# DeltaNet with unnormed keys: the keys' norm carried by beta and the values, the products of keys and queries three steps sooner

## The reference

```python
qkv = jax.nn.silu(centred_depthwise_conv(qkv, conv_w))      # 5 taps
q = l2norm(q.reshape(b_, s_, h_, HEAD_DIM)) * (HEAD_DIM ** -0.5)
k = l2norm(k.reshape(b_, s_, h_, HEAD_DIM))
beta = jax.nn.sigmoid(bt)
# chunk_gated_delta, forward and backward, chunks of tokens:
kb = k * beta[..., None]
a_low = jnp.where(strict, jnp.einsum("bhnid,bhnjd->bhnij", kb, k) * decay, 0.0)
rhs = jnp.concatenate([v * beta[..., None], kb * jnp.exp(gc)[..., None]], axis=-1)
sol = solve_triangular(a_low + eye, rhs)
attn = jnp.einsum("bhnid,bhnjd->bhnij", q, k) * decay
k_dec = k * jnp.exp(g_last - gc)[..., None]
...
o = rmsnorm(o_f + o_b, out_g) * silu(z)
```

## Time and profile before

| what | value |
|---|---|
| median of 3 runs | 2374.19 us (2373.24 to 2380.41) |
| the profiled execution's own time | 2374.28 us |
| its span, first to last instruction | 2372.5 us |
| mean granted TensorE clock | 0.998 |
| VectorE's first taps of k in groups 0, 1 and 2 | 167.30, 335.63, 504.91 us |

### The profile page before, as it was taken

One profiled execution on the slowest core, in us unless ns is written; L12 is line 12 of the kernel. 1 busy time (PEld: TensorE's weight loads), 2 busy tenths in 40 slices (PEclk: granted clock), 3 DMA queues, 4 the chain that ended last, 5 costly groups with the idle time before them and its releaser, 6 DMA issues.

```text
span 2372.5 us, 36123 instructions
## 1 busy us (share of the span) xinstructions
PE 2340.4 (99%) x11982; PEld 1982.2 (84%) x11982; DVE 1537.0 (65%) x2457; ACT 1250.9 (53%) x2326; POOL 159.9 (7%) x120
## 2 busy tenths in 40 slices
PE   8999999999999999999999999999999999999998
PEld 6887888988888888888888888888888888888886
DVE  6668778678676765556665565556676555676554
ACT  6656556565455554445554455555555444455544
POOL 0012002011001000001000000000111000011000
PEclk9999999999999999999999999999999999999999
DMA  9565355353366665666666666556666666666665
GB/s 335 156 169 151 107 143 142 107 177 98 103 177 189 189 191 193 194 188 186 186 189 193 193 208 172 162 184 197 185 185 186 194 193 191 186 186 186 194 192 172
DMA packets 234264, 423.00 MB, mean 178 GB/s; under 512 B 27532, under 2 KB 35613, under 8 KB 233501
## 3 DMA queue, kind: packets, MB, share of 16 engines
q1 hardware_dynamic: 234141, 421.33, 59.4%
HBM read 419.14 MB, written 2.10 MB: 178 GB/s over the span
## 4 chain that ended last, share of the span: by engine, by line
PE 94%; DVE 4%; ACT 1%; DMA 1%; issue 0%; SPq 0%; POOLq 0%; DVEq 0%; POOL 0%; ACTq 0%
PE pair L519 18%; PE pair L521 18%; PE pair L520 18%; PE pair L538 10%; PE aux L538 10%; PE aux L540 5%; PE pair L540 5%; PE aux L710 4%; PE aux L567 2%; DVE r L1768 1%; DVE w_lo L1540 1%; DMA raw<-in_mem_w_kv 1%; PE aux L750 0%; DVE r L1841 0%; PE aux L686 0%; PE aux L669 0%
## 5 line engine op out<-in xcount | busy, mean ns | idle before, releaser
L1540 DVE TENSOR_TENSOR w_lo<-raw,w_hi 128x512 fp32r<-128x512 f32 x1536 | 1090.8, 735 | 615.5 <-ACT w_hi L1026 613.1
L1026 ACT ACTIVATE w_hi<-raw 128x512 fp32r<-128x512 f32 x1536 | 938.6, 633 | 767.4 <-DMA raw<-in_ffn_w 626.6
L519 PE MATMUL pair<-w_hi,xT 128*128 128x512 f32 x960 | 386.9, 403 | 13.7 <-DVE w_lo L1540 10.4
L519 PE MATMUL pair<-w_hi,hid_hi 128*128 128x512 f32 x1012 | 394.4, 390 | 0.0
L521 PE MATMUL pair<-w_hi,hid_lo 128*128 128x512 f32 x1012 | 393.9, 389 | 0.0
L520 PE MATMUL pair<-w_lo,hid_hi 128*128 128x512 f32 x1012 | 393.7, 389 | 0.0
L521 PE MATMUL pair<-w_hi,xT 128*128 128x512 f32 x960 | 375.3, 391 | 0.0
L520 PE MATMUL pair<-w_lo,xT 128*128 128x512 f32 x960 | 374.6, 390 | 0.0
L538 PE MATMUL pair<-xT,w_hi 128*128 128x512 f32 x1024 | 362.6, 398 | 0.4 <-DVE h L2030 0.2
L538 PE MATMUL aux<-xT,w_hi 128*128 128x512 f32 x1024 | 360.8, 397 | 0.0
L540 PE MATMUL aux<-xT,w_lo 128*128 128x256 f32 x1024 | 287.4, 281 | 0.0
(11 more groups left out here) (244 smaller groups left out, 1593.8 us busy)
## 6 DMA issues: line engine op xcount, KB each, us to landing
raw<-in_ffn_w SPq DMA_DIRECT2D x1024, 256.0 KB, 3.0
raw<-in_dn_w_in SPq DMA_DIRECT2D x208, 256.0 KB, 2.9
raw<-in_tok_w_out SPq DMA_DIRECT2D x128, 256.0 KB, 3.0
raw<-in_gm_w_in SPq DMA_DIRECT2D x112, 256.0 KB, 2.9
raw<-in_mem_w_kv SPq DMA_DIRECT2D x64, 256.0 KB, 3.6
r<-in_mem_columns SPq DMA_DIRECT2D x8, 256.0 KB, 6.6
h<-in_x_columns SPq DMA_DIRECT2D x2, 1024.0 KB, 7.4
h<-in_mem_columns SPq DMA_DIRECT2D x8, 256.0 KB, 3.6
```

Of the source, the lines that this page charges most:

```text
L519: pe.matmul(acc, act_hi[:, kt, tokens], w_hi[:, slot], start=start, stop=False)
L1026: act.activation(w_hi[:, slot], raw[:, slot], ACT.Copy).then_inc(hi_ready, 1)
L1540: dve.tensor_tensor(w_lo[:, slot], raw[:, slot], w_hi[:, slot].bitcast(F32), ALU.subtract).then_inc(tiles_split, 1)
```

## The change

Keys stay unnormed. k after `silu` goes straight to `kqT`, and its transpose to tokens is used where normed k was. With r = 1 / (sum of squares of k + eps), `means` takes the reciprocal and multiplies beta by r; the values are multiplied by the root of the sum (`head_root`, GpSimd's power 1/2, used in `scaled_values` by VectorE, where ScalarE copied them). `decayed_keys` multiplies the unnormed keys by their decay out of the bank on VectorE, where VectorE wrote the normed keys and GpSimd scaled them. The transposes DE and their copies are gone. The gate products DF and the products DG come three steps sooner, the masking (L1835, L1841) is spread over two steps, and the taps of k and q over more steps in groups 0 and 1. The transposes of q and its squares move behind level 4 (`Q_LEVEL`, `DQ`), `query_term` to the end. `mix_pairs(2, 3)` stands behind the transposes DH. GpSimd's additions L2230 wait for half of k's squares and stand ahead of its power. A group has three steps fewer, and `ALONE` is `(22,)`.

```diff
 ORDER = (1, 0, 2)
-DA, DD, DE, DF, DG, DH, DI = 0, 6, 10, 12, 16, 20, 24
-V_LEVEL = 2
+DA, DD, DF, DG, DH, DI = 0, 6, 8, 12, 16, 20
+V_LEVEL, Q_LEVEL = 2, 4
 DV = DI + 6 * (V_LEVEL + 1)
-DFT = DI + 6 * len(LEVELS) + 2
+DQ = DI + 6 * (Q_LEVEL + 1) + 2
+DFT = DI + 6 * len(LEVELS) + 4
 DWV = DFT + 4
 DST, DO1, DKS, DQS, DWR, DO2 = DWV + 4, DWV + 6, DWV + 8, DWV + 10, DWV + 12, DWV + 14
...
-DMA0, DMA2 = DD + 2, DF
+DMA0, DMA2 = DF, DI
...
-ALONE = (19, 21, 23, 25)
+ALONE = (22,)
...
-                    src = kqT[:, 0] if X == 0 else conv[X]
+                    src = kqT[:, X] if X < 2 else conv[X]
...
                 mix_pairs(0, 1)
                 yield
-                yield
-                by_tokens(0, DD + 2)
-                yield
-                for _ in range(1 * roomy):
-                    yield
-                for m in range(2):
-                    have(DD + m)
-                for hp in range(2):
-                    pair_transposes(at(DE + hp), tok[:, 1], hp, rnd)
-                yield
-                mix_pairs(2, 3)
                 for f in range(4):
                     fill(DF + f)
                     pe.wait_ge(sem("gates_spread"), g * 4 + (f + 1))
@@ -751,8 +741,6 @@
                                    start=True, stop=True), DF + f)
                 yield
-                for n in range(2):
-                    have(DE + n)
                 pe.wait_ge(sem("silu_done"), g * 3 + 2)
                 for m in range(2):
                     for hp in range(2):
@@ -765,18 +753,16 @@
                         done(mm, n)
                 yield
                 yield
-                for d in range(2):
-                    for m in range(2):
-                        have(DG + 2 * m)
-                        have(DG + 2 * m + 1)
-                        transposes(at(DH + 2 * d + m), [(k * P, NT[:, d, m, k, :]) for k in range(4)], rnd)
-                yield
-                yield
                 for _ in range(1 * roomy):
                     yield
+                for m in range(2):
+                    have(DG + 2 * m)
+                    have(DG + 2 * m + 1)
+                    for d in range(2):
+                        transposes(at(DH + 2 * m + d), [(k * P, NT[:, d, m, k, :]) for k in range(4)], rnd)
+                yield
+                mix_pairs(2, 3)
+                yield
...
+                    if l == Q_LEVEL:
+                        by_tokens(0, DQ)
...
-                    pe.wait_ge(sem("kdec_done"), g * 2 + (d + 1))
+                    have(DD + d)
...
-                    if X == 2:
+                    if X == 2 and not roomy:
                         silu(1)
                     yield
+                if roomy:
+                    silu(1)
                 yield
                 for _ in range(1 * roomy):
                     yield
-                squares(1, (sq[:, 0], sq[:, 1]), DD)
+                squares(1, DD)
                 yield
                 mix_pairs(0, 1)
                 yield
                 silu(0)
-                yield
-                squares(0, v_new, DD + 2)
-                yield
-                for _ in range(1 * roomy):
-                    yield
-                for hp in range(2):
-                    n = DE + hp
-                    fil(n)
-                    free(act.activation(kqT[:, 1, 2 * hp:2 * hp + 2, :], halves(n), ACT.Copy), n)
-                attention_part()
-                yield
-                mix_pairs(2, 3)
                 for f in range(4):
                     drained(act, at(DF + f), rnd)
                     act.activation(NT[:, f // 2, f % 2], NT[:, f // 2, f % 2], ACT.Exp).then_inc(sem("decay_ready"), 1)
                 yield
                 yield
-                yield
+                attention_part()
+                yield
+                for _ in range(1 * roomy):
+                    yield
...
+                mix_pairs(2, 3)
+                yield
...
-                    if l == V_LEVEL:
-                        for m in range(2):
-                            fil(DV + m)
-                            free(act.activation(tok[:, 2, m], bank(DV + m)[:], ACT.Copy), DV + m)
+                    if l == Q_LEVEL:
+                        squares(0, DQ)
...
                     dve.tensor_scalar(ss[:, 1], ss[:, 1], 1.0, EPS, ALU.mult, ALU.add).then_inc(sem("head_means"), 1)
+                    dve.wait_ge(sem("head_means"), g + 1)
+                    dve.reciprocal(rs[:, 0], ss[:, 1]).then_inc(sem("head_inverse"), 1)
+                    dve.wait_ge(sem("head_inverse"), g + 1)
+                    dve.wait_ge(sem("group_gates"), g + 1)
+                    betas = gs[:, 2 * G_BETA:2 * G_BETA + 4, :].rearrange("p (m d) h -> p m d h", d=2)
+                    dve.tensor_tensor(betas, betas, rs[:, 0].unsqueeze(2).broadcast_to([P, 2, 2, 4]), ALU.mult
+                                      ).then_inc(sem("betas_scaled"), 1)
...
-                def normalise():
-                    dve.wait_ge(sem("head_rstd"), g + 1)
+                def decayed_keys():
+                    for d in range(2):
+                        n = DD + d
+                        fil(n)
+                        free(dve.tensor_tensor(kdec[d], heads(n), rows(gs[:, 2 * (G_EKD + d) + d, :], P), ALU.mult), n)
+                def scaled_values():
+                    dve.wait_ge(sem("head_root"), g + 1)
                     for m in range(2):
-                        n = DD + m
-                        free(dve.tensor_tensor(by_head(tok[:, 1, m]), heads(n), rows(rs[:, 1, m], P), ALU.mult), n)
+                        n = DV + m
+                        fil(n)
+                        free(dve.tensor_tensor(v_tok[m], heads(n), rows(rs[:, 1, m], P), ALU.mult), n)
                 dve.wait_ge(sem("padded"), g * 2 + 2)
                 convolve(1, 0, 1)
                 yield
-                convolve(1, 2, 3)
-                yield
-                convolve(0, 0, 1)
-                yield
-                convolve(0, 2)
-                yield
-                for _ in range(1 * roomy):
+                if roomy:
+                    convolve(1, 2)
+                    yield
+                    convolve(1, 3)
+                else:
+                    convolve(1, 2, 3)
+                yield
+                for i in range(3):
+                    convolve(0, i)
                     yield
                 convolve(0, 3)
+                mix_pairs(0, 1)
                 yield
                 means()
-                mix_pairs(0, 1)
-                yield
-                normalise()
-                yield
-                yield
-                for _ in range(1 * roomy):
-                    yield
-                query_term()
-                attention_part()
-                yield
-                mix_pairs(2, 3)
+                decayed_keys()
                 for f in range(4):
...
-                dve.wait_ge(sem("head_squares1"), g * 8 + 8)
+                dve.wait_ge(sem("betas_scaled"), g + 1)
...
+                    if m == 1:
+                        attention_part()
+                    yield
+                for _ in range(1 * roomy):
+                    yield
+                for m in range(2):
+                    n = DH + 2 * m
...
+                    if l == V_LEVEL:
+                        scaled_values()
...
+                query_term()
...
-                pool.wait_ge(sem("head_means"), g + 1)
-                pool.tensor_tensor(flat(rs[:, 1]), flat(ss[:, 1]), neg_half[:], ALU.pow).then_inc(sem("head_rstd"), 1)
+                pool.wait_ge(sem("head_squares1"), g * 8 + 4)
                 for f in range(4):
                     d, m = f // 2, f % 2
                     c = (C_BIGF, C_BIGB)[d]
                     pool.tensor_tensor(g_big[:, f], over(cst[:, c:c + P]), heads(gall[:, 2 * (G_GC + m) + d, g * 4:g * 4 + 4]), ALU.add
                                        ).then_inc(sem("gates_masked"), 1)
-                pool.wait_ge(sem("group_gates"), g + 1)
+                pool.wait_ge(sem("head_means"), g + 1)
+                pool.tensor_tensor(flat(rs[:, 1]), flat(ss[:, 1]), pos_half[:], ALU.pow).then_inc(sem("head_root"), 1)
                 for m in range(2):
                     have(DG + 2 * m)
                     have(DG + 2 * m + 1)
@@ -2237,9 +2229,6 @@
                     pool.tensor_tensor(dst, NT[:, 1, m], over(cst[:, C_M1L:C_M1L + P]), ALU.mult).then_inc(sem("x0_pool"), 1)
                     pool.wait_ge(sem("x0_pool"), g * 4 + (2 * m + 1))
                     pool.tensor_tensor(dst, dst, over(ident), ALU.add).then_inc(sem("x0_pool"), 1)
-                for d in range(2):
-                    pool.tensor_tensor(kdec[d], kdec[d], heads(gs[:, 2 * (G_EKD + d) + d, :]), ALU.mult
-                                       ).then_inc(sem("kdec_done"), 1)
...
```

(22 more changed lines are left out.)

4 lines of the change are left out of this document (1 added, 3 removed).

## The result

The changed kernel takes 2385.05 us (median of 6 runs, 2381.25 to 2389.14); beside it the kernel before took 2373.86 us. The ratio is 1.0049 (95%: 1.0037 to 1.0062), 11.2 us slower, where the forecast was 2376.5 and its range ended at 2383.5.

What follows compares the result with a forecast made beforehand. TensorE, busy 99% of the span, was taken as the bound. Terms -2.6 - 12.1 + 6.8 + 1.0 + 12x, with x = 0.76, gave +2.2 on 2374.28: 2376.5 us, range 2367 to 2383.5.

Steps and rivals of the forecast that it cites:

- The transposes: TensorE, all three groups: k is no longer transposed back, 24 transposes gone, 2.6 us less.
- The waits that go: TensorE, all groups: waits for low halves, masking and silu(2), among others, go with their hand-overs; 12.1 us less.
- The waits that come: Gate products DF on TensorE wait for decayed_keys: 1.2, 1.2 and 4.4 us, plus 9.1 from x; 15.9 us more.
- x: VectorE's loss for each of GpSimd's 12 additions beside taps and splits; taken as 0.76 us, 9.1 us in all.
- whole lock: Rival: VectorE's taps and GpSimd's additions exclude each other for whole instructions, x = 1.2; 2381.8 us; chance 0.17.
- not slowed: Rival: VectorE's taps are not slowed beside GpSimd, x near 0 to 0.3; 2367.4 to 2371 us; chance 0.20.
- Later in the third group: TensorE behind the gate products, up to the decay transposes and pair 2's bank: 1.0 us more, bounds 0 and 2.
- the masking wait: TensorE's waits from masking the products, at 225.44 and 558.63 before; counted as gone with masking halved over two steps.
- the third rival: Masking waits stay (1.07 twice, 0.56; +3.2 with hand-overs), or later waits reach 2 us; 2379.7 to 2381 us; chance 0.12.
- signs that the prediction named as right: Waits at 175.58, 179.95, silu(2) gone; gate products wait 3 to 5 us, third group 6 to 9; slower q taps.
- slower: Total slower by more than 0.3% (7.1 us): most of the whole lock and the top of the third rival; chance 0.19.

Runs made afterwards that it cites:

- pool_early: The changed kernel with GpSimd's four additions moved to the start of the group: 2369.0 us, ratio 0.9991 to the kernel before.
- keys_first_pool_early: The changed kernel with means and decayed_keys ahead of the third tap of q and GpSimd's four additions at the group's start: 2368.34 us, ratio 0.9976.
- slab_between: The changed kernel with TensorE's gate products one slab later, directly ahead of the key products: 2372.82 us, ratio 1.0008 to the kernel before.

## Why the prediction was wrong

- **The transposes** went, 24 of them, as forecast.
- **The waits that go** went: those at 175.58, 179.95 and 225.44, their like in group 1, 0.47, 0.35 and 0.56 in the third group, the one for `silu(2)` and three of the four of 0.30. The first of the third group stayed (0.54), as forecast.
- **The waits that come** have the place, the releaser and the size forecast: 4.29, 4.28, 7.33 against 4.2, 4.2, 7.4.
- **x** was 0.78 where 0.76 was taken from the splits' rows. A tap loses beside GpSimd what a split loses. The rivals "whole lock" (x = 1.2) and "not slowed" are both out. By the Trainium skill's rule ("SBUF — State Buffer", on who interferes with whom) the two would take turns for whole instructions. The rows come near to that: a tap of 0.40 us and an addition of 1.01 take 1.2 to 1.3 us for the pair, where one after the other would be 1.41. But the tap's loss, 0.78, is less than the whole addition, so a lock of all of it is not shown.
- **Later in the third group**: 0.98 and 1.07 us with two hand-overs of 0.16 make 2.4, where 1.0 was taken; the bound was 2. That is 1.4 us. The first of them stands ahead of the second decay transposes and starts as VectorE's masking ends, so the masking wait, counted as gone, had come back there: the third rival was right in this part.
- **The step that failed** is one sentence of the first part: "The granted clock is 0.998 over the span, the 2.4 GHz level, so it has no part." It was true of the DeltaNet stretch of the kernel before, whose longest wait there was 1.82 us, and it was carried over to a kernel whose waits are 4 to 7 us. The waits that come were priced at their length alone. The price is more. In group 0 the second four gate products and half a slab take 5.91 us (194.26 to 200.17), and 3.21 in pool_early at the full clock (190.65 to 193.86): 2.7. Group 1 is the same. In the third group the eight gate products take 5.25 us (536.93 to 542.18) where they took 3.03 before (535.57 to 538.60): 2.2. Together **7.6 us** that no term held.

The sum again: forecast +2.2, clock +7.6, later waits +1.4, makes +11.2; the groups grew by 10.4 and the medians by 11.2. That the last digit agrees is luck: the hand-overs of the three new waits, 0.5 us, are not in the sum. All signs that the prediction named as right did come, since none of them looked at the matmuls behind the wait. The forecast had chosen the likeliest time by a chain of work in which each product has one price; the price depended on the state in which the wait left the engine. The chance of "slower" (0.19) hung on a dearer x and on later waits, and not on this.

What stays open is when a wait brings the clock down. In the groups, waits of up to 1.86 us and one of 3.06 did not; 2.00, 2.89, 3.12, 3.15, 3.95, 4.19 and all longer ones were followed by half-rate matmuls; 3.31 us did so in one group and not in the other. Nor do its length and the work ahead of it settle the question. Ahead of the groups, where all these kernels are alike, TensorE waits 1.5 us for the gates in every trace. In seven of the thirteen the matmuls that follow are 0.43 us apart for a while, in six they are not, the kernel before among them. TensorE's timeline, after:

```profile
95.63 0.59 PE L652 MATMUL aux<-gall,cst 128*128 128x12 f32 x4 [1.52 <-DVE gall L1669]
...
98.37 0.63 PE L522 MATMUL pair<-w_lo,xT 128*128 128x512 f32 x1
98.80 0.63 PE L523 MATMUL pair<-w_hi,xT 128*128 128x512 f32 x1
```

From that wait to the next transposes it is 5.76 us in after and 4.20 in before: 1.6 us of clock outside the groups, which one execution pays and another does not. How often the six runs behind each median paid it, no run here shows. That also limits the forecast for a single kernel: some 1.5 to 3 us behind each wait of 1.5 to 4 us, taken or not.

## What to carry to other kernels

When TensorE is the bound and runs at its full clock, price a new wait of several us at its length and some 2 to 3 us behind it (1.8 to 3.1 behind waits of 4.28 to 7.42 us here; every wait of 3.95 us and more was followed by matmuls at half rate, and some of the shorter ones, down to 1.5 us), and ask of the sum whether the new order turns many short waits into one long one: here thirteen short ones (10 us) went, three long ones came (16 us), and the clock behind the long ones made up most of the loss. Look beside VectorE's chain as well as along it: GpSimd's four additions, put elsewhere than beside the taps, gave back 5 to 6 us in each of groups 0 and 1, where the taps had lost 3.1. A wait that is taken away moves to the next bank or buffer that is late: count the chain two or three releases on before writing down a gain.

## What the runs showed that was not expected

- Adding work to TensorE made the kernel faster: 2377.75 us with the waits filled against 2385.05 (the kernel before took 2373.02 and 2373.86 beside them), with 10 more matmuls in each of groups 0 and 1 and more transposes in the third.
- Behind a wait of 2.00 us the matmuls were 0.43 us apart for some 3 us (537.40 to 540.29 in keys_first_pool_early); behind one of 3.06 us in slab_between the clock stayed at 1.00, and behind the same 1.5 us for the gates it fell in seven traces of thirteen.
- The half rate doesn't begin with the wait: in after the clock was still 1.00 at 192 to 193 us, when TensorE had been idle since about 190, and it lasted until 199.9, that is 5.6 us into the work that followed.
